# Rotary step of queries and keys: four DMA copies inside SBUF in place of a matmul with a signed permutation

## The reference, cut to what matters

```
def rope(x, pos):
    half = D_HEAD // 2
    inv = ROPE_THETA ** (-jnp.arange(half, dtype=jnp.float32) / half)
    ang = pos.astype(jnp.float32)[:, None] * inv[None, :]
    cos = jnp.cos(ang)[:, None, None, :]
    sin = jnp.sin(ang)[:, None, None, :]
    xf = x.astype(jnp.float32)
    x1, x2 = xf[..., :half], xf[..., half:]
    return jnp.concatenate([x1 * cos - x2 * sin, x2 * cos + x1 * sin], axis=-1).astype(x.dtype)
...
    q = rope(rms_norm(q, p['q_norm_g']), pos)
    k = rope(rms_norm(k, p['k_norm_g']), pos)
```

## Time and profile before

| what | value |
|---|---|
| runs | 3821.68, 3828.18, 3830.54 us; median 3828.18 |
| span of the profiled execution | 3819.9 us, 66230 instructions |
| PE busy | 3750.9 us, 98% |
| DVE busy | 3018.9 us, 79% |
| ACT, POOL busy | 1103.6 us (29%), 1283.5 us (34%) |
| DMA | 1285.55 MB, mean 337 GB/s |

### The profile page before, as it was taken

How to read it: one execution, slowest core, us unless ns; L and a number is a source line. 1 busy time by engine, 2 the same in 40 slices (tenths; PEclk the granted TensorE clock), 3 DMA queues, 4 the chain that set the end, 5 groups by cost and what they waited for, 6 DMA issues and landing times.

```text
span 3819.9 us, 66230 instructions
## 1 busy us (share of the span) xinstructions
PE 3750.9 (98%) x24811; PEld 3702.8 (97%) x24811; DVE 3018.9 (79%) x3613; ACT 1103.6 (29%) x1124; POOL 1283.5 (34%) x929
## 2 busy tenths in 40 slices
PE   7999999999999999999999999999999999999999
PEld 7999999999999998999999999999999999999999
DVE  7887788778865544688789999997588888888886
ACT  4333333232321112322333333332222222222221
POOL 4344344333444442455442222223022222222220
PEclk9999999999999999999999999999999999999999
DMA  7899898998889989999989999999889989898995
GB/s 297 288 323 339 311 308 288 339 334 290 305 297 303 351 328 323 377 374 367 373 325 395 381 386 387 381 383 395 300 317 354 358 325 358 324 342 338 341 359 197
DMA packets 451706, 1285.55 MB, mean 337 GB/s; under 512 B 34369, under 2 KB 258369, under 8 KB 343361
## 3 DMA queue, kind: packets, MB, share of 16 engines
q1 hardware_dynamic: 372576, 876.99, 64.3%
q0 software_dynamic: 46080, 335.56, 22.3%
q10 hardware_dynamic: 32832, 70.07, 4.7%
HBM read 1070.18 MB, written 345.75 MB: 371 GB/s over the span
## 4 chain that ended last, share of the span: by engine, by line
PE 55%; issue 27%; POOL 13%; DMA 2%; DVE 2%; ACT 1%; SPq 0%; POOLq 0%; ACTq 0%; DVEq 0%
PE ST L2051 27%; PE ST L1974 18%; POOL w_lo L686 13%; PE PA L1974 4%; PE PA L1687 3%; PE ST L2027 2%; DMA rows<-u_rows,v_idx 1%; DMA w_raw<-w_all 1%; DVE w_lo L1031 1%; DVE h_lo L1040 1%; DMA u_rows<-u_out 1%; ACT w_hi L749 0%; PE PA L1936 0%; SPq L509 0%; DVE PA L1583 0%
## 5 line engine op out<-in xcount | busy, mean ns | idle before, releaser
L686 POOL TENSOR_TENSOR w_lo<-w_raw,w_hi 128x512 fp32r<-128x512 f32 x588 | 816.8, 1420 | 1078.1 <-ACT w_hi L749 1046.9
L749 ACT ACTIVATE w_hi<-w_raw 128x2048 fp32r<-128x2048 f32 x368 | 704.2, 1914 | 1321.0 <-PE ST L2051 645.7
L2051 PE MATMUL ST<-wt_hi,w_hi 128*128 128x384 f32 x2048 | 684.6, 334 | 0.5 <-DVE w_lo L1031 0.5
L2051 PE MATMUL ST<-wt_hi,w_lo 128*128 128x384 f32 x2048 | 684.1, 334 | 0.0
L2051 PE MATMUL ST<-wt_lo,w_hi 128*128 128x384 f32 x2048 | 684.1, 334 | 0.0
L1031 DVE TENSOR_TENSOR w_lo<-w_raw,w_hi 128x2048 fp32r<-128x2048 f32 x220 | 503.4, 2288 | 150.6 <-ACT w_hi L749 143.3
L1687 PE MATMUL PA<-h_hi,w_hi 128*128 128x272 f32 x2464 | 529.3, 296 | 5.2 <-DVE w_lo L1031 5.2
L722 POOL DMA_INDIRECT rows<-v_rows,v_idx x160 | 252.4, 1577 | 790.0 <-DVE PA L1583 717.6
L1687 PE MATMUL PA<-h_hi,w_lo 128*128 128x272 f32 x2464 | 511.4, 289 | 0.0
L1687 PE MATMUL PA<-h_lo,w_hi 128*128 128x272 f32 x2464 | 509.8, 288 | 0.0
L1974 PE MATMUL ST<-h_hi,w_hi 128*128 128x384 f32 x1408 | 508.4, 361 | 0.9 <-DVE w_lo L1031 0.9
(11 more groups left out here) (284 smaller groups left out, 6139.1 us busy)
## 6 DMA issues: line engine op xcount, KB each, us to landing
w_raw<-w_all SPq DMA_DIRECT2D x368, 1024.0 KB
u_in<-w_all SPq DMA_DIRECT2D x128, 1024.0 KB, 8.6
u_rows<-u_out SPq DMA_DIRECT2D x512, 256.0 KB, 7.6
v_rows<-w_all SPq DMA_DIRECT2D x128, 1024.0 KB, 11.3
a_scr<-gb ACTq DMA_DIRECT2D x128, 192.0 KB, 6.7
g_scr<-g_st ACTq DMA_DIRECT2D x24, 1024.0 KB
gl_st<-g_scr SPq DMA_DIRECT2D x30, 768.0 KB, 10.6
a_st<-a_scr SPq DMA_DIRECT2D x30, 768.0 KB
```

What stands on the lines that cost most here:

```text
L686: ins = pool.tensor_tensor(w_lo[:, slot, cols], raw[:, slot, cols], w_hi[:, slot, cols].bitcast(F32), ALU.subtract)
L749: act.activation(w_hi[:, slot, :], raw[:, slot, :], ACT.Copy).then_inc(hi_ready, 1)
L2051: last = mm(PB[n % 2][:, k, :], a, r_[b][:, c, :], start=(c == 0 and y == 0), stop=(c == GRP - 1 and y == 2))
```

## The change

`rot` leaves PE. In the slots of queries and keys ACT issues four DMAs on its own queue, each of 32 partitions by 544 values (68 KB), from `xg` into `e_row`, which is the start of the tile `e` that the softmax uses later in the head. They swap the two halves of each vector. The minus signs of the first halves are put into the sine table once at the start, by two DVE instructions. DVE then multiplies from SBUF by the sines in two instructions, where it took three from PSUM. `values` (the transposes of v) waits for the last `oraw` of the head before in place of `rot_taken`.

```
+        e_row = e[:, :, :].rearrange("p c n -> p (c n)")[:, 0:T]
...
                 if i in (0, 1):
+                    act.wait_ge(tr_ready, h * STEPS + 1)
+                    act.wait_ge(z_taken, h * 7 + (i + 1))
+                    for q in range(4):
+                        to, fr = q * 32, (q ^ 1) * 32
+                        act.dma_start(e_row[to:to + 32, :], xg[fr:fr + 32, :]).then_inc(rot_ready, 16)
                     act.wait_ge(stat_ready, h * 3 + (i + 2))
                     std(1.0 / DH)
...
             dve.wait_ge(const_loaded, 32)
+            for q in (0, 64):
+                sin = cst[q:q + 32, C_SIN:C_SIN + TP]
+                own.by(V.tensor_scalar(sin, sin, -1.0, None, ALU.mult))
...
-                dve.wait_ge(rot_ready, h * 2 + (i + 1))
+                dve.wait_ge(rot_ready, h * 128 + 64 * (i + 1))
                 for to, fr in cs:
                     own.by(V.tensor_tensor(xg[:, to], xg[:, to], cst[:, fr], ALU.mult))
-                s0, t0 = C_SIN, TP - HT
-                own.by(V.tensor_tensor(sq[:, 0:HT], TO[:, 0, 0:HT], cst[:, s0:s0 + HT], ALU.mult))
-                own.by(V.tensor_tensor(sq[:, HT:TP], TO[:, 1, 0:t0], cst[:, s0 + HT:s0 + TP], ALU.mult))
-                V.tensor_tensor(sq[:, TP:T], TO[:, 1, t0:HT], cst[:, s0 + PAST:s0 + PAST + TS], ALU.mult).then_inc(rot_taken, 1)
-                dve.wait_ge(rot_taken, h * 2 + (i + 1))
+                for to, fr in cs:
+                    own.by(V.tensor_tensor(sq[:, to], e_row[:, to], cst[:, C_SIN + fr.start:C_SIN + fr.stop], ALU.mult))
+                settle()
...
-            def rot(h, i):
-                pe.wait_ge(z_taken, h * 7 + (i + 1))
-                if i == 0:
-                    pe.wait_ge(o_ready, h * STEPS + 1)
-                else:
-                    pe.wait_ge(rot_taken, h * 2 + i)
-                spread(TO, perm, xg).then_inc(rot_ready, 1)
-
             def values(h, j):
                 pe.wait_ge(zb_full, h * ZPH + 5)
-                pe.wait_ge(rot_taken, h * 2 + 2)
+                pe.wait_ge(o_ready, h * STEPS + 1)
...
-                at = {(1, 1 + by): lambda: stats(h, 0), (1, 2 + by): lambda: rot(h, 0),
-                      (2, 1): lambda: stats(h, 1), (2, 2): lambda: rot(h, 1),
+                at = {(1, 1 + by): lambda: stats(h, 0), (2, 1): lambda: stats(h, 1),
```

More of the change, by code:

```diff
@@ L312, in build @@
         sq_ready, stat_ready, std_ready = sem("sq_ready"), sem("stat_ready"), sem("std_ready")
-        rot_ready, rot_taken, norm_done = sem("rot_ready"), sem("rot_taken"), sem("norm_done")
+        rot_ready, norm_done = sem("rot_ready"), sem("norm_done")
         vt_ready, v_ready = sem("vt_ready"), sem("v_ready")
@@ L1693, in _ @@
             blk = cst[:, C_BLK:C_BLK + P]
-            perm = cst[:, C_PERM:C_PERM + P]
             ones = cst[:, C_ONES:C_ONES + P]
```

## The result

The changed kernel's median is 3873.06 us (3868.88 to 3875.15, 4 runs), that of the kernel before 3825.57 us on the same chip: ratio 1.0127, 95% interval 1.0115 to 1.0139. That is 47 us more, and slower where no measurable change was forecast. The profiled span went from 3819.9 to 3871.6 us, and all of it is lost in the z stage. (In the runs that have both, the time of a launch is 1.8 us above its profiled span. So most of the 8.3 us that the text ahead of the prediction puts down to starting and ending the program was spread between executions; the forecast of a change of 5.8 us does not depend on it.)

What follows compares the result with a forecast made beforehand. It took PE to bound heads 2, 4, 6 and the loop of DMA store, turn and `evac` the first units of heads 0, 1, 3, 5, 7. Head terms -1.8 + 4.5 + 0.3 + 2.8 = +5.8 us gave 3834.0 us, range 3817 to 3848.

Steps and rivals of the forecast that it cites:

- What bounds the kernel, and what is removed: Z stage: PE or the store loop sets the pace by head; 14.7 us of PE work removed, an upper bound.
- Traffic: Z stage's full DMA stretches: each exchange pushes store landings back 0.73 us, 1.5 us a head.
- ACT's queue: Issues ahead of `rstd`: keys 0 to 0.6 us later, most queries unaffected, head 0's query 2.0 us later.
- Latency: DVE's wait for the fourth DMA: landing 7 us after `xg` (3.1 to 10.9), 0.6 us wait per key slot.
- sign of a wrong forecast: DVE waiting over 1.5 us in each key slot, or the stores' landings not moving.
- Rival 2: Exchange lands late, 9 us after `xg`, DVE waiting 2.6 us per key slot: 14.5 us lost, 3843; chance 0.28.
- Sum by heads: Z stage: heads 2, 4, 6 -1.8; 1, 3, 7 +4.5; 5 +0.3; 0 +2.8; sum +5.8 us.
- The clock: PE after longer waits for `sq`: half clock expected in heads 0, 1, 3, 7, costing 1.7 us each; head 5 already has it.
- Rival 3: Half clock lasts 6.8 us in five heads after waits over 3 us: 14.3 us lost, 3842; chance 0.13.

Runs made afterwards that it cites:

- no_exchange: Changed kernel without any exchange, DVE multiplying `xg` itself by the sines: 3823.8 us, ratio 0.9995.
- idle_small_slot2: Kernel before plus four DMAs of 32 x 16 per slot that DVE never waits for, ACT's wait for them in its third slot: 3850.7 us, ratio 1.0053.
- act_unrolled: Changed kernel with ACT's loop over the four pairs of heads written out, so no jump back: 3868.0 us, ratio 1.0113.
- behind_std: Changed kernel with the four exchange DMAs moved behind the root on ACT: 3903.1 us, ratio 1.0194.
- copies_behind_unrolled: Changed kernel with four ACT copies behind the root in place of the DMAs, and ACT's loop written out: 3827.2 us, ratio 1.0001.
- one_dma: Changed kernel with one DMA of 128 x 544 in place of four, halves not swapped: 3846.7 us, ratio 1.0047.
- idle_one: Kernel before plus one DMA of 128 x 544 per slot that DVE never waits for, ACT's wait for it ahead of the first exponential: ratio 1.0039.
- idle_one_slot2: Kernel before plus one DMA of 128 x 544 per slot that DVE never waits for, ACT's wait for it in its third slot: 3833.6 us, ratio 1.0016.
- act_copies: Changed kernel with four ACT activations from `zb` in place of the DMAs, ahead of the root: 3853.9 us, ratio 1.0077.

## Why the prediction was wrong, step by step

- **What bounds the kernel, and what is removed.** Right. 14.7 us of PE work were worth 2 us (no_exchange); heads 2, 4 and 6 gained 1.8, 1.8 and 1.5 us there, and the others moved by -0.7 to +0.7.
- **Traffic.** No error that matters. Over the whole, the stores were waited for less (76.4 us), since DVE stood elsewhere; four small DMAs cost what four full ones cost, within the intervals.
- **ACT's queue. This is the step that failed**: "The fourth issue starts 1.0 to 2.0 us after the first", and "`rstd` waits there for PE over 2 us anyway, so nothing comes of it". The short price was 0.34 us an issue; the row of 0.6 us, a copy inside SBUF as this one is, was the nearer neighbour, though four of those make 2.4 us, and the four took 2.4 to 4.9, on average 3.7. For the queries, 2.8 to 4.8 us plus the 1.28 us load is more than the time that the root waited for: it starts 5.0 us after `xg` in even heads' queries (2.8 before) and 5.7 in odd ones (3.8). In odd heads DVE is in a turn then, and indeed little comes of it (14.7 to 15.3 us); in even heads DVE stood idle 6.2 to 10.2 us for the root (1.3 to 3.8 before), part of it for the gap at the jump. In head 0, where the prediction had the root 2.0 us later (1.4 to 2.6), it was 5.0. For the keys "0 to 0.6 us" was 2.3 us in even heads and 1.1 in odd ones. Of the 39.9 us by which the products came later, counted from `xg`, idle_small_slot2 has 20.4 from the issues alone; copies ahead of the root in place of behind it cost some 22 us.
- **Latency.** The form was right and the size was off. "I take 7", with 3.1 to 10.9: the mean landing was 10.3, 10.8, 12.2 and 8.9 us after `xg` (kinds of slot as in the table). A landing from its own issue was near the row (6.6 against 6.2 us), but the fourth was issued 2.6 us after `xg` on average in place of 1 to 2, and landed 8.0 us after its own issue, later than its three predecessors. DVE's waits in key slots were 1.3 to 2.6 us, in seven of eight over the 1.5 that was named as a sign of a wrong forecast, and at least four query slots waited too. The other 19.5 us, by subtraction only, are left for this. Rival 2 ("lands late") named it, but with 14.5 us as price, since it let only key slots pay.
- **Sum by heads.** The heads that were to gain (2, 4, 6: -1.8) lost 27.4 us (23.4 in act_unrolled, without the gap); 1, 3 and 7 lost 14.3 for 4.5; 5 lost 2.6 for 0.3; 0 lost 9.2 for 2.8. In the even heads the slack of 2.3 us at the scores was right, but the path goes by the query: its late product holds up the key's `evac`, and in heads 2, 4 and 6 PE waits 3.5 to 5.2 us for `sq` at the keys' sums, where it did not wait before.
- **The clock.** The drops came: 61 us at half clock up to 1500 us against 20 before, among them this one in head 2 (columns as in the earlier trace rows). They follow from the waits and add to them: behind_std has 99 us. Rival 3 was right in kind. Here such a stretch, behind a wait of PE:

```profile
333.40:340.10 6.70, 6.19 (x23) 5.73 (x24) 2.61 (x2) 3.61 (x4) 3.73 (x4) 0.50 0.85 282
```

- **Not seen at all.** The gap at ACT's jump back. It makes `xg` of heads 2, 4 and 6 late by 13.6 us together. Writing the loop out shortened the z stage by 11 of its 54 us, and the median by 5.

So the 14 us by which the z stage lost more than its 16 slots are mostly that gap: in act_unrolled, without it, the slots lose 42.4 us and the z stage 42.9. What stays open is what the clock alone cost, since every run changes the waits and the clock together, and how much of the loss by the medians is the gap (5 us, with intervals that overlap).

The Trainium skill ("DMA: Bandwidth & Descriptors", Anatomy of one DMA) would have had the exchange done in an estimated 2.6 us; the page gives its figures for DMAs that GpSimd issues, and here ACT issued them. The last of the four landed 8.0 us after its own issue and 8.9 to 12.2 us after `xg` (means), so the rows of this kernel were the ones to go by.

## What to carry to other kernels

An instruction that issues a DMA is work of its engine: price it by the row of the same kind of transfer, and put it into the chain of what stands behind it in order, table loads too. Before moving work from a nearly full engine to one busy for 29%, follow the slot's chain through all engines; here 0.92 us a slot saved on the full engine gave 2 us in all, and 3 us a slot on the idle one, ahead of the root, cost 22 us more than nearly the same behind it. If the work must go there, put it behind what others wait for; copies_behind_unrolled, which did, costs nothing and gains nothing either, since the rest of the chain was no shorter.

## What was not expected of the hardware

- An issue on ACT's queue took a median of 0.63 us for a DMA of 32 x 544 and 0.64 us for one of 32 x 16, but 0.48 us for one of 128 x 544; single ones of the four took up to 2.25 us. SP's took 0.64 us.
- With some instructions more in its loop, ACT stood 4.1 to 5.7 us after each of three jumps back, where it stood 0.2 us before; with only a few more (one_dma, idle_one) it did not. That it fetches its instructions anew is only argued, but the profile's packets on the second queue for instructions were 92 or 93 in all nine kernels with the gap and 77 to 82 in the nine without.
- Adding a wait ahead of an activation can move its table load behind the wait: 1.3 us in each of 8 heads, 0.23% (9 us) between idle_one and idle_one_slot2.
- ACT writes to other partitions than it reads: four copies of 32 x 544 shifted by 32 took 2.70 to 3.06 us, where issuing four DMAs took 2.4 to 4.9, and DVE never waited for them in act_copies.
